# Low parts of the output weights made early and kept in DRAM, projections stretched to step 636, the second token group of the output after attention

## The reference

```python
h = rmsnorm(x, a_norm)
q, k, v, g = split(h @ w_in, 4)              # w_in: 1024 x 4096
z = q_h @ k_h.T / 8                          # per head, keys s < t only
w[t, s] = sigmoid(z[t, s]) * prod_{s<j<t} (1 - sigmoid(z[t, j]))
o = w @ v_h
x = x + (o * silu(g)) @ w_out                # w_out: 1024 x 1024
out = rmsnorm(x, final_norm)
```

## Time and profile before

| what | us |
|---|---|
| three runs | 1689.11, 6259.58, 1689.63 (median 1689.63) |
| the profiled execution, its own time | 1687.99 |
| its span in the profile | 1686.3 |
| values | to about 188 |
| attention, steps 0 to 639 | about 215 to 1525.8 |
| output alone | 1526.5 to the end |

### The profile page before, as it was taken

How to read it: one execution, slowest core, us unless ns; L and a number is a source line. 1 busy time by engine, 2 the same in 40 slices (tenths; PEclk the granted TensorE clock), 3 DMA queues, 4 the chain that set the end, 5 groups by cost and what they waited for, 6 DMA issues and landing times.

```text
span 1686.3 us, 23240 instructions
## 1 busy us (share of the span) xinstructions
PE 1653.6 (98%) x8600; PEld 1377.5 (82%) x8600; DVE 1328.6 (79%) x1871; ACT 899.5 (53%) x1765; POOL 262.5 (16%) x220
## 2 busy tenths in 40 slices
PE   7999999999999999999999999999999999989998
PEld 6888878888888888888888888888888888778886
DVE  4534378888888888888988988888888898986763
ACT  6633255655655555655565656565655556652221
POOL 0020012110111021101120112012201111306600
PEclk9999999999999999999999999999999999999999
DMA  9854434352424242333333333434252426369631
GB/s 306 269 149 146 125 114 137 94 144 69 150 75 132 70 148 95 119 98 116 101 104 105 104 120 94 123 99 129 63 152 81 125 69 219 122 197 329 232 138 62
DMA packets 159329, 224.50 MB, mean 133 GB/s; under 512 B 49392, under 2 KB 90352, under 8 KB 159216
## 3 DMA queue, kind: packets, MB, share of 16 engines
q1 hardware_dynamic: 89728, 147.44, 27.4%
q10 hardware_dynamic: 69488, 75.58, 15.0%
HBM read 147.39 MB, written 75.56 MB: 132 GB/s over the span
## 4 chain that ended last, share of the span: by engine, by line
PE 87%; DVE 5%; DMA 3%; issue 2%; ACT 1%; SPq 1%; POOL 0%; ACTq 0%; DVEq 0%
PE proj_ps L677 27%; PE turn_ps L704 12%; PE proj_ps L637 10%; PE o_ps L718 7%; PE o_ps L719 7%; PE z_ps L695 7%; PE z_ps L694 7%; PE turn_ps L745 4%; PE z_ps L745 3%; PE proj_ps L745 3%; DVE u L1069 2%; DVE r_turned_lo L1074 1%; PE o_ps L745 1%; DMA v_next<-v_rows 1%; DMA gate<-gate_cols 1%
## 5 line engine op out<-in xcount | busy, mean ns | idle before, releaser
L853 ACT ACTIVATE u<-z_ps 128x512 f32<-128x512 f32 (+3 forms) x640 | 341.0, 533 | 421.0 <-PE z_ps L695 416.8
L1069 DVE TENSOR_TENSOR_SCAN u<-u,u 128x512 f32<-128x512 f32 x384 | 497.8, 1296 | 0.0
L1074 DVE TENSOR_TENSOR r_turned_lo<-turn_ps,r_turned_hi 128x512 fp32r<-128x512 f32 (+3 forms) x640 | 376.9, 589 | 38.9 <-ACT r_turned_hi L859 37.5
L859 ACT ACTIVATE r_turned_hi<-turn_ps 128x512 fp32r<-128x512 f32 (+3 forms) x640 | 340.0, 531 | 64.0 <-issue 45.5
L609 POOL TENSOR_SCALAR w_raw<-w_raw,a_norm_col 128x128 f32<-128x128 f32 x192 | 178.9, 949 | 1184.6 <-DMA w_raw<-in_w_qkg 1184.6
L704 PE MATMUL turn_ps<-ident,u 128*128 128x128 f32 x2176 | 343.8, 273 | 0.0
L677 PE MATMUL proj_ps<-hT_hi,w_hi 128*128 128x512 f32 x768 | 319.8, 416 | 0.0
L677 PE MATMUL proj_ps<-hT_lo,w_hi 128*128 128x512 f32 x768 | 319.6, 416 | 0.0
L677 PE MATMUL proj_ps<-hT_hi,w_lo 128*128 128x512 f32 x768 | 319.6, 416 | 0.0
L704 PEld LDWEIGHTS turn_ps<-ident,u 128*128 128x128 f32 x2176 | 268.3, 140 | 59.7 <-issue 0.4
L718 PE MATMUL o_ps<-r_turned_hi,dv_head 128*128 128x512 f32 (+3 forms) x640 | 233.0, 364 | 14.3 <-DVE r_turned_lo L1074 13.3
(11 more groups left out here) (105 smaller groups left out, 1641.8 us busy)
## 6 DMA issues: line engine op xcount, KB each, us to landing
x_T<-in_xT SPq DMA_DIRECT2D x32, 512.0 KB, 5.2
qk_hi_cols<-made_hi ACTq DMA_DIRECT2D x64, 256.0 KB, 2.5
qk_lo_cols<-made_lo ACTq DMA_DIRECT2D x64, 256.0 KB, 3.1
w_raw<-in_w_qkg SPq DMA_DIRECT2D x24, 512.0 KB, 3.5
x_rows<-in_x SPq DMA_DIRECT2D x16, 512.0 KB, 4.3
v_rows<-v_stage ACTq DMA_DIRECT2D x32, 256.0 KB
v_here<-v_rows SPq DMA_DIRECT2D x64, 128.0 KB, 2.9
v_next<-v_rows SPq DMA_DIRECT2D x64, 128.0 KB, 2.9
```

The lines of the kernel that those rows point to most:

```text
L853: nc.scalar.activation(u_t[(m // CB) % RU][STEPS[m][3]][:, 0:w], z_ps[m % RZ][:, 0:w], ACT.Sigmoid, scale=-Z_SCALE).then_inc(s_u, 1)
L859: nc.scalar.activation(rt_hi[m % RT][:, 0:w], t_ps[m % RT][:, 0:w], ACT.Copy).then_inc(s_hi, 1)
L1069: nc.vector.tensor_tensor_scan(u, u, other, start, ALU.mult, op).then_inc(s_r, 1)
L1074: nc.vector.tensor_tensor(rt_lo[m % RT][:, 0:w], t_ps[m % RT][:, 0:w], as_f32(rt_hi[m % RT][:, 0:w]), ALU.subtract).then_inc(s_lo, 1)
```

## The change

1. During the second half of the values SP loads w_out's eight row blocks once (load_out_weight, from loop step 4), ACT and DVE make the high and the low part in three stages of buffers (steps 5 to 12), and SP stores the low part to a new DRAM tensor, w_out_lo_rows (steps 6 to 13). SP keeps two x_T loads ahead, and loads w_raw 0 and 1 at step 1 and not 3.
2. POOL's eight subtractions are gone. w_out and its stored low part are both loaded from step 623 on (16 DMAs of 512 KB instead of 8), and ACT makes the high part in place, one block in each of steps 627 to 634.
3. The filling goes at 677/200 = 3.385 a step; the last eight groups are reordered, and the last is complete in step 636.
4. OUT_FROM is 637: 18 matmuls of group 0 are in attention's steps (6 in each of the last three), 78 come after it. Group 1 is loaded at 637, and its pieces are at 643, 644, 645, 647, behind attention's last step, in the loops of ACT and DVE, which now run to step 651.

By the constants of the code:

| | before | after |
|---|---|---|
| chunks 0 and 1 of hT free after step | 590 | 622 |
| chunk 2, chunk 3 free after | 604, 618 | 600, 636 |
| loads of w_out | 591 | 623 |
| group 0 loaded (first k tiles; last) | 605 (7); 619 (1) | 601 (6); 619 (2) |
| group 1 loaded | 619 | 637 |
| PIECE_STEP, group 0 | 610, 612, 614, 621 | 605, 609, 613, 623 |
| PIECE_STEP, group 1 | 624, 626, 628, 630 | 643, 644, 645, 647 |
| put_out from | 624 | 637 |
| group 2 loaded at | 631 | 638 |

The diff, cut to its core:

```diff
+AT_WSTAGE = [(BASE + a * KB, BASE + b * KB) for a, b in ((16, 24), (20, 28), (84, 76))]
+RW = len(AT_WSTAGE)
...
-    return order + [(first, 0), (first, 1), (last, 0), (last, 1), (first, 2), (last, 2), (first, 3), (last, 3)]
+    return order + [(first, 2), (first, 0), (last, 2), (last, 0), (first, 1), (last, 1), (first, 3), (last, 3)]
...
-FILL_NUM, FILL_DEN = 697, 200
+FILL_NUM, FILL_DEN = 677, 200
...
+WO_AT = {WO_FROM + k: k for k in range(KT)}
...
-REST_FROM = max(DONE[NG - 1] + 1, NS - HS + 4 * CB + 3)
+LAST_K_FROM = NS - HS + 4 * CB + 3
+REST_FROM = DONE[NG - 1] + 1
 PIECE = 2
 PIECES = KT // PIECE
-PIECE_STEP = [SHORT_FROM + 5, SHORT_FROM + 7, SHORT_FROM + 9, REST_FROM + 2] + [REST_FROM + 5 + 2 * i for i in range(PIECES)]
+PIECE_STEP = [SHORT_FROM + 4, SHORT_FROM + 8, SHORT_FROM + 12, LAST_K_FROM + 4] + [REST_FROM + at for at in (6, 7, 8, 10)]
+LAST_PIECE_STEP = PIECE_STEP[-1] + 4
 SUM_AT = {n: i for i, n in enumerate(PIECE_STEP)}
 GATE_AT = {n + 2: i for i, n in enumerate(PIECE_STEP)}
 LOW_AT = {n + 4: i for i, n in enumerate(PIECE_STEP)}
-OUT_FROM = REST_FROM + 5
+OUT_FROM = REST_FROM
...
+        wo_raw = place(nc, "wo_raw", [P, KT, D], F32, AT_WO_HI)
         wo_lo = place(nc, "wo_lo", [P, KT, D], F32R, AT_WO_LO)
-        wo_raw = place(nc, "w_out_raw", [P, KT, D], F32, AT_WO_LO)
+        stage_raw = [place(nc, f"w_out_raw{n}", [P, D], F32, at[0]) for n, at in enumerate(AT_WSTAGE)]
+        stage_lo = [place(nc, f"w_out_lo{n}", [P, D], F32R, at[1]) for n, at in enumerate(AT_WSTAGE)]
+        stage_hi = [place(nc, f"w_out_hi{n}", [P, D], F32R, at[1]) for n, at in enumerate(AT_WSTAGE)]
...
+                def load_out_weight(k):
+                    if k == 0:
+                        sp.wait_ge(s_sumsq, NB)
+                    if k >= RW:
+                        sp.wait_ge(s_wost[k % RW], 16 * (k // RW))
+                    sp.dma_start(stage_raw[k % RW][:], w_out[k * P:(k + 1) * P, :]).then_inc(s_woraw[k % RW], 16)
+                def store_out_weight(k):
+                    rows = slice(k * P, (k + 1) * P)
+                    sp.wait_ge(s_wolo, k + 1)
+                    sp.dma_start(wo_low_parts[rows, :], as_f32(stage_lo[k % RW][:])).then_inc(s_wost[k % RW], 16)
+                def out_weights_stored(k):
+                    for n in range(RW):
+                        sp.wait_ge(s_wost[n], 16 * len(range(n, k + 1, RW)))
...
+                load_xT(NB)
+                load_xT(NB + 1)
                 for s in range(NB):
-                    load_xT(NB + s)
-                    if s == 3:
+                    if s == 1:
                         sp.wait_ge(s_v, NB)
                         load_w(0)
                         load_w(1)
+                    if 0 <= s - 6 < KT:
+                        store_out_weight(s - 6)
+                    if 0 <= s - 4 < KT:
+                        load_out_weight(s - 4)
+                    if s + 2 < NB:
+                        load_xT(NB + s + 2)
+                out_weights_stored(KT - 1)
...
-                    if WO_FROM <= n < WO_FROM + KT:
-                        k = n - WO_FROM
+                    if n in WO_AT:
+                        k = WO_AT[n]
                         if k == 0:
                             sp.wait_ge(s_p, GROUP_OF["g", KT - 1, 1] + 1)
-                        sp.dma_start(wo_raw[:, k, :], w_out[k * P:(k + 1) * P, :]).then_inc(s_woraw[k], 16)
+                        rows = slice(k * P, (k + 1) * P)
+                        sp.dma_start(wo_raw[:, k, :], w_out[rows, :]).then_inc(s_woagain[k], 16)
+                        sp.dma_start(as_f32(wo_lo[:, k, :]), wo_low_parts[rows, :]).then_inc(s_wolow, 16)
                     if n == SHORT_FROM:
                         sp.wait_ge(s_p, GROUP_OF["g", KT - 1, 2] + 1)
-                        sp.wait_ge(s_gst, stores_through(GROUP_OF["g", KT - 1, 0]))
+                        sp.wait_ge(s_gst, stores_through(GROUP_OF["g", LAST_G - 1, NC - 1]))
                         for par in range(2):
-                            sp.wait_ge(s_oout[par], 32 * (H - 2) * NC // 2)
-                        load_group(0, slice(0, KT - 1), s_in[0])
+                            sp.wait_ge(s_oout[par], 32 * 2 * LAST_G * NC // 2)
+                        load_group(0, slice(0, LAST_G), s_in[0])
                     if n == SHORT_FROM + 2:
                         for b in range(2):
                             load_xy(b)
+                    if n == LAST_K_FROM:
+                        sp.wait_ge(s_gst, stores_through(GROUP_OF["g", KT - 1, 0]))
+                        chunk_stored(0)
+                        load_group(0, slice(LAST_G, KT), s_first)
                     if n == REST_FROM:
-                        chunk_stored(0)
-                        load_group(0, slice(KT - 1, KT), s_first)
                         sp.wait_ge(s_p, NG)
                         load_group(1, slice(0, KT), s_in[1])
                         sp.dma_start(norm_row[:], final_norm.rearrange("(a n) -> a n", a=1).to_broadcast([P, D])).then_inc(s_nrow, 16)
-                    if n == NS - LEAD_SCORES:
+                    if n == NS - 2:
...
-                for k in range(KT):
-                    pool.wait_ge(s_wohi, k + 1)
-                    nc.gpsimd.tensor_tensor(wo_lo[:, k, :], wo_raw[:, k, :], as_f32(wo_hi[:, k, :]), ALU.subtract).then_inc(s_wolo, 1)
...
-                            pe.wait_ge(s_wolo, KT)
+                            pe.wait_ge(s_woparts, KT)
+                            pe.wait_ge(s_wolow, 16 * KT)
+                            pe.wait_ge(s_plo, NG - 1)
+                        if i == QPM:
                             pe.wait_ge(s_plo, NG)
...
+                def out_weight_hi(k):
+                    act.wait_ge(s_woraw[k % RW], 16 * (k // RW + 1))
+                    nc.scalar.activation(stage_hi[k % RW][:], stage_raw[k % RW][:], ACT.Copy).then_inc(s_wohi, 1)
+                def out_weight_high(k):
+                    act.wait_ge(s_woagain[k], 16)
+                    nc.scalar.activation(wo_hi[:, k, :], wo_raw[:, k, :], ACT.Copy).then_inc(s_woparts, 1)
...
+                    if 0 <= s - 5 < KT:
+                        out_weight_hi(s - 5)
+                act.wait_ge(s_wolo, KT)
...
-                    k = (n - WO_FROM - 3) // 2
-                    if (n - WO_FROM) % 2 and 0 <= k < KT:
-                        act.wait_ge(s_woraw[k], 16)
-                        nc.scalar.activation(wo_hi[:, k, :], wo_raw[:, k, :], ACT.Copy).then_inc(s_wohi, 1)
+                    if n - 4 in WO_AT:
+                        out_weight_high(WO_AT[n - 4])
...
+                def out_weight_lo(k):
+                    dve.wait_ge(s_wohi, k + 1)
+                    nc.vector.tensor_tensor(stage_lo[k % RW][:], stage_raw[k % RW][:], as_f32(stage_hi[k % RW][:]),
+                                            ALU.subtract).then_inc(s_wolo, 1)
...
+                    if 0 <= s - 5 < KT:
+                        out_weight_lo(s - 5)
```

More of the change, by code:

```diff
@@ L241, in rms_chain, with all_stages @@
     return count
-def all_stages(nc, x, xT, a_norm, w_v, w_qkg, w_out, v_dram, qk_hi, qk_lo, g_dram, o_hi, o_lo,
+def all_stages(nc, x, xT, a_norm, w_v, w_qkg, w_out, wo_low_parts, v_dram, qk_hi, qk_lo, g_dram, o_hi, o_lo,
                          final_norm, out):
@@ L365, in all_stages @@
         s_ost = sem("o_evacuated")
-        s_woraw = sems("w_out_raw_loaded", KT)
+        s_woraw = sems("w_out_raw_loaded", RW)
         s_wohi = sem("w_out_hi_ready")
         s_wolo = sem("w_out_lo_ready")
+        s_wost = sems("w_out_parts_stored", RW)
+        s_woagain = sems("w_out_loaded", KT)
+        s_woparts = sem("w_out_hi_made")
+        s_wolow = sem("w_out_lo_loaded")
         s_oout = sems("o_stored", RO)
@@ L962, in _ @@
                     v_stored(act, v)
-                for n in range(-LEAD_SCORES, NS + 2):
+                for n in range(-LEAD_SCORES, LAST_PIECE_STEP + 1):
                     ended = chunk_end(n - 1) if inside(n - 1) else None
@@ L974, in _ @@
                         store_made(g)
-                    for g in GROUPS_DONE[n]:
+                    for g in GROUPS_DONE.get(n, []):
                         made_high(g)
@@ L1208, in stick_breaking_layer @@
     o_lo = scratch("o_lo_cols", [D, S], F32)
-    all_stages(nc, x, xT, a_norm, w_v, w_qkg, w_out, v_dram, qk_hi, qk_lo, g_dram, o_hi, o_lo, final_norm, out)
+    wo_low_parts = scratch("w_out_lo_rows", [D, D], F32)
+    all_stages(nc, x, xT, a_norm, w_v, w_qkg, w_out, wo_low_parts, v_dram, qk_hi, qk_lo, g_dram, o_hi, o_lo, final_norm, out)
 def kernel(**inputs):
```

## The result

The changed kernel takes 1679.99 us (median of 4 runs, 1677.71 to 1680.63), the kernel before 1689.75; the ratio is 0.9941, 95% interval 0.9929 to 0.9953. The profiled execution took 1680.25 us with a span of 1678.5, 7.8 us under the span of before. The forecast was 1677.5, its range 1669 to 1687. One of the four runs of the kernel before took 6259.58 us; the ratio is made without it.

The account below looks back on a forecast made before the run. PE, busy 98% of the span, was taken as the bound. 17.3 - 1.0 - 1.8 - 3.0 - 0.2 = 11.3 us less gave 1676.7 from the profiled execution, 1678.3 from the median; forecast 1677.5, range 1669 to 1687.

Parts of the forecast that it names:

- (b): Last head, group 0's first pieces at 605 and 609: DVE crowded after the load, 1.0 us lost, 0.8 for small waits elsewhere.
- (c): From step 622, 16 w_out loads for 8: ACT stands, put_out waits at 637; 2.0 us waiting plus 1.0 clock, 3.0 lost.
- (a): Steps 0 to 600: less filling brings PE sooner to where DVE is late, so waits grow; 1.0 us lost.
- Gain: Last head's excess of 16.9 us comes back, plus 0.4 from 78 put_out matmuls moved behind attention: 17.3 us.
- POOL's share: Last head: POOL's eight subtractions hold up DVE's scans in steps 594 to 612; removing them returns about 7 us.
- The gap and the pieces: Last head from step 619: no filling while DVE is crowded with both groups' pieces; removing this returns 10 us.
- (d): Group 1 loaded and prepared after attention: ready at T + 14 (T: attention's end), 4 us cover for block 1; 0.2 us lost.
- (f): The rest, groups 2 to 7 behind attention: group 2 due later, at T + 40 (T: attention's end), tail the same; no cost.
- group 1 is not ready: Rival, 8%: behind attention, a later load and POOL's sum delay group 1's last low part; PE waits 2.6 us, total 1682.
- (e): Second half of the values: added DMA, ACT and DVE work for w_out is hidden, cost 0, cover 4 us without that.
- The burst is late by more: Rival, 17%: w_out loads run as at 340 GB/s, PE waits 4.5 us at step 637 plus 1.7 clock; 1684.
- the full gain: Rival, 10%: DMA reaches 400 GB/s, no new wait, only less-filling cost and small waits stay; 1671 us.

Follow-up runs that it names:

- stored_low_late: Kernel before in its own order, stored low parts of w_out loaded instead of POOL's subtractions, all issued at step 599 behind v's last loads: 1683.38 us, ratio 0.9965.
- pool_in_new_order: Changed kernel, but POOL again subtracts w_out's low parts in place and only eight blocks are loaded: 1685.63 us, ratio 0.9975 to the kernel before.
- three_together: Changed kernel with first pieces at 607 and 610, w_out's blocks loaded ahead of the low parts, and one-tensor-input norm products: 1671.52 us, ratio 0.9895.
- the values part alone: Kernel before plus w_out split beside the values, low part stored but not read, end as before: 1690.14 us, ratio 1.0001.
- raws_first: Changed kernel with the 16 loads at step 623 reordered, w_out's eight blocks first, then the eight low parts: 1682.22 us, ratio 0.9956 to the kernel before.
- one_input_chain: Changed kernel with the norm's three 128 x 1 products taking one tensor and a per-partition scalar operand: 1676.35 us, ratio 0.9920 to the kernel before.
- pieces_later: Changed kernel with group 0's first two pieces at steps 607 and 610 instead of 605 and 609: 1678.24 us, ratio 0.9931 to the kernel before.
- stored_low_alone: Kernel before in its own order, low parts loaded instead of subtracted by POOL, 16 loads from step 591, two a step: 1693.02 us, ratio 1.0022.

## Why the prediction was right, step by step

**The sum.** Forecast 11.3 us less, measured 7.8 in the profile (span) and 9.8 in the medians. In the profile's terms the 3.5 us of difference are: head 15 gave 1.1 less than the sum has with (b) and (c) in it (11.0 for 12.1), the time behind attention cost 3.7 more, the start 0.8 more, and (a), which was to cost 1.0, gave 1.1. So the mechanism of the gain was right and one cost was missed; that the sum came out as near as it did is in part luck, since an error of 2.1 the other way lies in it.

**Gain, 16.9 + 0.4 expected.** Head 15 shortened by 11.0 us beyond its filling; 5.9 of the excess is still there, where (b) and (c) had 4.8. Of the two causes, POOL's share was put at 7 us and is 6 (stored_low_late) or 5.6 (pool_in_new_order, undone). The gap and the pieces were put at 10 and were not tested by themselves; what the new order gives with POOL still in it is 4, and in that trace it pays (b), POOL's waits at put_out and 2.0 us behind attention. With the costs of (b), (c) and (d) mostly taken out again the whole change is worth 18.4 us (three_together, 1689.88 less 1671.52) where the gain was put at 17.3.

**(a) Less filling in the heads, 1.0 expected.** Not seen: heads 0 to 14 are 1.1 us shorter than the shift of filling explains. The waits there stand at other steps than before (1.4 us in step 560, where before had none), but their sum is no greater (3.1 us, before 3.2). The prediction named as a sign of being wrong that the other heads do not fall from 80 to 78.6 us. Heads 0 to 14 did, from 79.9 to 78.9 in the mean; head 14 alone did not (80.3 for 79.6), by the wait in its step 560. Weigh of step 0 came 0.8 us later; the values part alone shows that too (231.5) with no change in its total, so I make nothing of it.

**(b) First pieces, 1.0 and 0.8 expected.** The mechanism was right, the size too small: DVE stood 2.67 us, and PE lost 2.8 us in three waits (2.04, 0.17, 0.62), with some 0.6 in slower steps around them. What was mis-sized is the load. Its third and last request, the gate's, took 10.1 us to land where I had 8.3, and it was made 1.3 us behind the first, which I had not counted: 11.4 us in all, 1416.39 to 1427.8. Before, the same three requests of seven k tiles took 10.5 us, so a smaller load did not land sooner. The two loads of x and a gate store run beside it in both kernels and do not explain that; the cause stays open.

**(c) The burst, 3.0 expected.** PE lost 1.83 us and no clock. The cause is the forecast one, ACT in line behind loads of w_out. The place is not: I let ACT's two steps of lead cover everything up to put_out's wait in step 637, and overlooked the copy of attention's output for chunk 2, which stands in the same line at step 636 and has no lead at all. The burst as such was in time for step 637 in raws_first and 1.0 us late in three_together.

**(d) and (f) Behind attention, 0.2 expected, 3.9 measured.** This is the step that failed. Group 1 was in time, as worked out: its last low part ended 14.7 us behind weigh(639) (I had T + 14), PE went through its 96th matmul without a pause, and the rival "group 1 is not ready" did not come true. "The rest: group 2 is due at T + 40; the tail is the same" was wrong. I compared the due times of groups with the arrival of loads, and not DVE's line, which also has the banks of block 2 to empty.

Two things meet there. The first is time. POOL's first add begins at 1513.5, 45 us ahead of the time at which PE comes to block 6 (1558.6); before, it began at 1516.6, 54 us ahead of it (1570.3). The second is standing. From that add to block 2's residual DVE took 46.3 us, and before 36.1. In the changed kernel 17 us of it are standing under POOL's adds, 15 of them in five operations of one element for each partition (0.16 us each by themselves); before it was 7. SP requested group 3's load 4.1 us behind group 2's (1499.85 and 1503.93), where before it was 15.8 us (1505.13 and 1520.92), so POOL goes from one group to the next with a pause of 0.7 us and not 8.4, and the norm of block 0, which ran in that pause, now falls under the adds. Of the kernel before, POOL and DVE:

```profile
1533.31 5.62 POOL L618 TENSOR_TENSOR o_part_hi<-o_part_hi,o_part_lo 128x2048 f32<-128x2048 f32 x1 [8.37 <-DMA gate<-gate_cols]
```

```profile
1532.39 0.16 DVE L237 TENSOR_TENSOR stat<-stat 128x1 f32<-128x1 f32 x1
1532.59 0.16 DVE L238 TENSOR_TENSOR stat<-stat 128x1 f32<-128x1 f32 x1
...
1552.72 1.28 DVE L1109 TENSOR_TENSOR x_again<-z_ps,x_again 128x512 f32<-128x512 f32 x2
```

I had given the holding-up under POOL a price in the pieces, its right mechanism in the wrong place. The Trainium skill (SBUF — State Buffer, Who interferes with whom) has a VectorE instruction with two SBUF inputs contend with a GpSimd one that reads SBUF, and one with at most one SBUF input, outside the two-port modes, not at all; the trace agrees for products of one element (4.53 us against 0.21 us). The smallest tile is not spared.

**(e) The values, 0 expected.** Right, shown by itself. A full share was estimated at 300 GB/s; in 170 to 180 of the changed kernel 329 GB/s were moved at a share of 0.97. Over 110 to 180 the share was 0.79, not near 1.

**The rivals.** "The burst is late by more" did not happen; nor did the full gain, though three_together, at 1671.5, is what the full gain named (1671).

## What to carry to other kernels

- When work is moved from the steps to behind them, take each engine's whole line there, item by item, and not only the due time of the data: the cost came from an engine with a third of its time free (busy for 41 of the 64 us from 1496 to 1560), whose small operations stood under another's large ones.
- A wait for a load in an in-order engine costs what stands behind it with the least lead; look for the one item without a lead (here the copy that frees an accumulator).
- A fix that removes one wait and shows nothing is not yet shown to be wrong: look in the trace for where the time went, and test it again with the next wait on the path gone. The order of the loads is such a case, and an open one: alone it took 1682.2 us for 1680.0, with the others 1671.5 for 1673.8, and in neither pair are the intervals apart.

## What the runs showed of the hardware that was not expected

- A 128 x 1 product of two SBUF tensors took 0.16 us alone and up to 4.53 us beside POOL's adds; with one tensor and a scalar operand for each partition, also in SBUF, it took 0.21 us in all cases seen.
- Waits of PE of nearly the same length do not cost the same: behind 1.86 us (before, step 600), 1.90 us (one_input_chain, step 606), 1.92 us (raws_first, step 560) and 2.00 us (pieces_later, step 636) ten microseconds had a granted clock of 0.83, behind 2.04 and 1.83 us (changed kernel) it was 1.00. Each time 1.7 us hang on that, and what decides it no run here shows.
- A request of 128 KB behind 12 of 512 KB in one queue landed after 17.3 us (stored_low_alone), where the median of such requests in that kernel is 3.2 us.
